# The first slab of the convolution and of the second feed-forward taken from x scaled by its gain, with the token factor and the shift applied to the product

## What is computed

```python
def rms_norm(x, gain):                 # over the features of each token
    return x * rsqrt(mean(x * x, axis=-1) + 1e-6) * gain
def modulate(x, shift, scale):
    return x * (1 + scale) + shift

ax = modulate(rms_norm(hx, norm_mix[1]), sh1, sc1)
b_gate, c_gate, xv = split(ax @ w_in, 3)
hx = hx + g1 * ((b_gate * short_conv(c_gate * xv, w_conv)) @ w_out)
fx = modulate(rms_norm(hx, norm_ffn[1]), sh2, sc2)
hx = hx + g2 * ((silu(fx @ w1) * (fx @ w3)) @ w2)
```

## Time and profile before

| | us |
|---|---|
| median of 3 runs | 2349.04 (2348.41 to 2349.38) |
| the profiled execution | 2346.38 |
| its span | 2344.7 |
| TensorE busy | 2243.8 (96%) |
| VectorE busy | 1129.1 (48%) |
| ScalarE busy | 729.9 (31%) |
| mean granted TensorE clock | 0.979 of full speed |

### The profile page before, as it was taken

The page is one execution under the profiler, slowest core; times in us unless marked ns, Lnnn a source line. Parts: engine busy times, 40 slices in busy tenths (PEclk is TensorE's granted clock), DMA queues, the critical chain, the costliest instruction groups (busy, mean ns, idle before and its releaser), DMA issues.

```text
span 2344.7 us, 25372 instructions
## 1 busy us (share of the span) xinstructions
PE 2243.8 (96%) x9752; PEld 1748.0 (75%) x9752; DVE 1129.1 (48%) x1420; ACT 729.9 (31%) x951; POOL 29.4 (1%) x60
## 2 busy tenths in 40 slices
PE   6999999999899999989989999999999988999996
PEld 4868677686588888868868888887758876878875
DVE  7645343544577333253653323347868647422424
ACT  3221121212343122131233312234555534323321
POOL 0000000000000000000000000000000000000000
PEclk7999999999999999999999999999899999999998
DMA  7232322323187322222212222223201111222220
GB/s 313 72 121 89 121 72 76 120 86 117 61 298 272 108 90 89 92 74 104 90 72 90 100 98 90 89 90 106 72 1 37 37 36 59 102 90 90 90 105 39
DMA packets 32748, 231.88 MB, mean 99 GB/s; under 512 B 3760, under 2 KB 4016, under 8 KB 5552
## 3 DMA queue, kind: packets, MB, share of 16 engines
q1 hardware_dynamic: 23904, 171.98, 20.8%
q0 software_dynamic: 6912, 50.33, 5.7%
q10 hardware_dynamic: 1872, 8.73, 1.0%
HBM read 228.93 MB, written 2.10 MB: 99 GB/s over the span
## 4 chain that ended last, share of the span: by engine, by line
PE 90%; DVE 6%; ACT 2%; issue 1%; DMA 1%; DVEq 0%; POOL 0%; ACTq 0%; POOLq 0%
PE PS L470 26%; PE PS L471 26%; PE PS L472 26%; PE PS L593 4%; PE PS L584 2%; DVE rv L1614 1%; PE PS L848 1%; PE PS L942 1%; PE PS L813 1%; PE PS L932 1%; DVE cv L1967 1%; DMA ada_raw<-ada 1%; DVE w_lo L1511 1%; PE PS L503 0%; PE PS L779 0%
## 5 line engine op out<-in xcount | busy, mean ns | idle before, releaser
L1511 DVE TENSOR_TENSOR w_lo<-raw,w_hi 128x2048 fp32r<-128x2048 f32 x162 | 371.0, 2290 | 670.6 <-ACT w_hi L1072 670.5
L470 PE MATMUL PS<-act_hi,w_hi 128*128 128x512 f32 x1632 | 654.7, 401 | 34.6 <-DVE act_lo L1524 23.4
L1072 ACT ACTIVATE w_hi<-raw 128x2048 fp32r<-128x2048 f32 x162 | 310.1, 1915 | 1105.9 <-PE PS L472 1095.7
L471 PE MATMUL PS<-act_lo,w_hi 128*128 128x512 f32 x1632 | 648.9, 398 | 0.0
L472 PE MATMUL PS<-act_hi,w_lo 128*128 128x512 f32 x1632 | 648.5, 397 | 0.0
L470 PEld LDWEIGHTS PS<-act_hi,w_hi 128*128 128x128 f32 x1632 | 308.8, 189 | 116.6 <-issue 36.9
L471 PEld LDWEIGHTS PS<-act_lo,w_hi 128*128 128x128 f32 x1632 | 308.8, 189 | 76.2 <-issue 1.9
L472 PEld LDWEIGHTS PS<-act_hi,w_lo 128*128 128x128 f32 x1632 | 308.6, 189 | 75.8
L470 PE MATMUL PS<-hid_hi,w_hi 128*128 128x512 f32 (+1 forms) x672 | 266.1, 396 | 0.9 <-ACT sg L1472 0.9
L472 PE MATMUL PS<-hid_hi,w_lo 128*128 128x512 f32 (+1 forms) x672 | 265.4, 395 | 0.0
L471 PE MATMUL PS<-hid_lo,w_hi 128*128 128x512 f32 (+1 forms) x672 | 265.4, 395 | 0.0
(11 more groups left out here) (358 smaller groups left out, 2197.5 us busy)
## 6 DMA issues: line engine op xcount, KB each, us to landing
raw<-slabs SPq DMA_DIRECT2D x162, 1024.0 KB, 4.8
ada_raw<-ada POOLq DMA_DIRECT2D x44, 1024.0 KB, 5.1
early_raw<-ada POOLq DMA_DIRECT2D x4, 1024.0 KB, 21.2
toep<-decay ACTq DMA_DIRECT2D x5, 768.0 KB, 4.2
x<-x_t ACTq DMA_DIRECT2D x1, 2048.0 KB, 9.6
out_t<-x SPq DMA_DIRECT2D x4, 512.0 KB, 2.6
rs<-ctx_t ACTq DMA_DIRECT2D x1, 1024.0 KB, 14.1
con<-consts ACTq DMA_DIRECT2D x1, 642.0 KB, 4.0
```

The lines of the kernel that those rows point to most:

```text
L470: pe.matmul(o, w[0], a[0], start=first, stop=False)
L471: pe.matmul(o, w[0], a[1], start=False, stop=False)
L1072: act.activation(w_hi[:, n % 2, :], raw[:, n % 2, :], ACT.Copy).then_inc(w_hi_done, 1)
L1511: dve.tensor_tensor(w_lo[:, k % 2, :], raw[:, k % 2, :], w_hi[:, k % 2, :].bitcast(F32), ALU.subtract).then_inc(w_lo_done, 1)
```

## The change

For the first slab of the convolution and that of layer 1's feed-forward, the moving operand is no longer the finished normalisation but x times its gain (`xg_hi`, `xg_lo`), which needs no root. Since the token factor `rstd` is common to all features of a token, the product is multiplied by it afterwards. The shift has to go through the same weights: two more moving columns hold it (one would do; two keep the count even), and their result, one value for each output feature, is added as a bias. As 514 columns exceed a bank, each tile is done in two halves of 256 and 258 columns, in two banks. The second slab and all that follow use `act_hi` and `act_lo` as before.

- TensorE: `first_pair` in place of the first turn of `up`. It takes the k in the order in which x is finished. The three sums of squares move from behind the slab before into the first slab, behind its fifth step (`s == KT // 2`), and into bank 6.
- ScalarE: `scaled` (a copy with the gain as scale) ahead of each square. In the first place the rounding of the second slab goes between the last `scaled` and the last square, in the second place ahead of the root. `first_pair` applies the function with the summed shift as bias.
- VectorE: `scaled_rest` behind the additions, and the gains made ahead of them (`block_gain`). `first_pair` copies the shift's sum, multiplies two halves for each tile by `rstd`, and only then makes `w_lo` of the third slab.
- The last output slab of the convolution signals its first tile on its own (`tile_summed`), and its two additions wait for one tile each. `summed` keeps the later counts right.

```diff
+            def first_pair(n, name, order, banks, freed):
+                parts, after_x = 8 * nth_split(name + "_x"), 8 * nth_split(name)
+                pe.wait_ge(w_lo_done, n + 1)
+                pe.wait_ge(banks, freed[0])
+                for s, k in enumerate(order):
+                    pe.wait_ge(lo_ready, parts + s + 1)
+                    for m in range(2):
+                        w = wcols(n, k * 256 + m * P, k * 256 + (m + 1) * P)
+                        for half in range(2):
+                            at = slice(half * H, (half + 1) * H + 2 * half)
+                            mm = product(PS[:, BANK_X[name][m][half], 0:H + 2 * half], w, (xg_hi[:, k, at], xg_lo[:, k, at]),
+                                         s == 0, s == KT - 1)
+                    if s == KT // 2:
+                        pe.wait_ge(banks, freed[2])
+                        gathered_sum(nth(name), 6)
+                mm.then_inc(slab_done, 1)
+                pe.wait_ge(w_lo_done, n + 2)
+                pe.wait_ge(banks, freed[1])
+                tile_pair(n + 1, BANK_X[name][2], act, lo_ready, after_x).then_inc(slab_done, 1)
...
-                up(CONV, KT, FT, parts_of("mix1"))
+                first_pair(CONV, "mix1", FIN, down_added, (KT + 4, KT + 6, KT + 8))
+                up(CONV, KT, FT, parts_of("mix1"), 1)
...
-                swiglu(FFN1, FT + KT, 16, parts_of("ffn1"), None)
+                first_pair(FFN1, "ffn1", range(KT), wout_added, (4 + 6, 4 + 8, 4 + 8))
+                swiglu(FFN1, FT + KT, 16, parts_of("ffn1"), 1)
...
+            def first_pair(n, seen, step, func=ACT.Silu):
+                after_static(n)
+                for m in range(2):
+                    act.wait_ge(x_scaled, step + m + 1)
+                    act.activation(sg[:, m, :], sg[:, m, :], ACT.Identity if func == ACT.Copy else func,
+                                   bias=shift_sum[:, m:m + 1]).then_inc(act_silu, 1)
+                after_static(n + 1)
...
-                norm("mix1", mod_at(1, 0), CONV - 1, FIN, down_added, 8)
-                up(CONV, KT, FT, ACT.Copy)
+                for s, k in enumerate(FIN):
+                    act.wait_ge(down_added, KT + s + 1)
+                    scaled("mix1", s, k)
+                    if s == KT - 1:
+                        after_static(CONV - 1)
+                    square(nth("mix1"), s, x[:, k, :])
+                root(nth("mix1"), T, D, 6)
...
+                    scaled("ffn1", k, k)
                     square(nth("ffn1"), k, x[:, k, :])
-                root(nth("ffn1"), T, D)
                 after_static(FFN1 - 1)
+                root(nth("ffn1"), T, D, 6)
...
+            def first_pair(n, seen, name, conv=False):
+                b = BANK_X[name]
+                dve.wait_ge(slab_done, n + 1)
+                dve.wait_ge(act_silu, seen + 2)
+                for m in range(2):
+                    dve.tensor_copy(shift_sum[:, m:m + 1], PS[:, b[m][1], H:H + 1])
+                    dve.tensor_tensor(sg[:, m, 0:H], PS[:, b[m][0], 0:H], rstd[:, 0:H], ALU.mult)
+                    dve.tensor_tensor(sg[:, m, H:T], PS[:, b[m][1], 0:H], rstd[:, H:T], ALU.mult).then_inc(x_scaled, 1)
+                static_rest(n + 2)
...
+                    if norm and s:
+                        scaled_rest(norm, s - 1, FIN[s - 1])
                     if norm and 2 <= s <= 6:
                         gather(norm, s - 1)
```

More of the change, by code:

```diff
@@ L124, in build @@
         eps = sb("eps", [P, 3])
+        shift_sum = sb("shift_sum", [P, 2])
         std = sb("std", [P, T])
@@ L372, in build @@
         gathered = ("mix1", "ffn1", "post2", "last")
-        split = [q for q in norms if q not in ("final", "post2", "last")]
+        split = ["mix0", "ctx", "ffn0", "mix1_x", "mix1", "ffn1_x", "ffn1", "pre2", "ffn2"]
         def nth(name):
@@ L700, in two_turns, with finish_two_turns @@
                         mm.then_inc(slab_done, 1)
-            def finish_two_turns(n, moving, ready, before, free, norm):
+            def finish_two_turns(n, moving, ready, before, free):
                 for j in range(4):
@@ L1175, in after_static, with scaled, up @@
                     round_slab(n + 2)
-            def up(n, tiles, seen, func=ACT.Silu):
-                with act.Fori(0, tiles // 2) as i:
+            def scaled(name, s, k):
+                g = 3 if name == "mix1" else 4
+                if s == 0:
+                    act.wait_ge(gain_done, g + 2)
+                    at = mod_at(1, 0 if name == "mix1" else 3)
+                    act.activation(xg_hi[:, :, T:T + 2], mod[:, at:at + KT].unsqueeze(2).to_broadcast([P, KT, 2]), ACT.Copy)
+                act.activation(xg_hi[:, k, 0:T], x[:, k, :], ACT.Copy, scale=gain[:, g, k:k + 1]).then_inc(hi_ready, 1)
+            def first_pair(n, seen, step, func=ACT.Silu):
[5 more added lines that the diff above has]
+                after_static(n + 1)
+                for m in range(0 if func == ACT.Copy else 2):
+                    act.wait_ge(hraw_ready, seen + m + 3)
+                    act.activation(hid_hi[:, m, :], hraw[:, m, :], ACT.Copy).then_inc(hid_hi_done, 1)
+            def up(n, tiles, seen, func=ACT.Silu, done=0):
+                with act.Fori(done, tiles // 2) as i:
                     after(n, i)
@@ L1723, in static_rest, with scaled_rest @@
                     rest_slab(n, n)
-            def up(n, tiles, seen, unit0=None, conv=False):
-                with dve.Fori(0, tiles // 2) as i:
+            def scaled_rest(name, s, k):
+                g = 3 if name == "mix1" else 4
+                dve.wait_ge(hi_ready, 8 * nth_split(name + "_x") + s + 1)
+                if s == 0:
+                    at = mod_at(1, 0 if name == "mix1" else 3)
+                    dve.tensor_tensor(xg_lo[:, :, T:T + 2], mod[:, at:at + KT].unsqueeze(2).to_broadcast([P, KT, 2]),
+                                      xg_hi[:, :, T:T + 2].bitcast(F32), ALU.subtract)
+                dve.scalar_tensor_tensor(out=xg_lo[:, k, 0:T], in0=x[:, k, :], scalar=gain[:, g, k:k + 1],
+                                         in1=xg_hi[:, k, 0:T].bitcast(F32), op0=ALU.mult, op1=ALU.subtract).then_inc(lo_ready, 1)
@@ L1728, in up @@
+            def up(n, tiles, seen, unit0=None, conv=False, done=0):
+                with dve.Fori(done, tiles // 2) as i:
                     if unit0 is not None:
```

108 lines of the change are left out of this document (76 added, 32 removed).

## The result

| | before | after |
|---|---|---|
| median, us | 2348.72 (2347.16 to 2349.38, 4 runs) | 2311.02 (2306.89 to 2316.77, 4 runs) |
| profiled execution, us | 2346.38 | 2306.89 |
| its span, us | 2344.7 | 2305.2 |
| mean granted TensorE clock | 0.979 | 0.981 |

The account below looks back on a forecast made before the run. The prediction took TensorE, busy 90% of the span, as the bound, with gains only where it stands still. Savings of 4.5 and 3.65 us in two places made 8.15: median 2349.04 to 2340.9 us, range 2338 to 2346.

Parts of the forecast that it names:

- Part 1: First slab's matmuls in both places: half matmuls 0.118 us apart, 1.42 us a step, 11.3 us a slab.
- rival D: Half matmuls of the first slabs bound by weight loads, 0.233 us apart: slower, 2354.5 us; chance 0.05.
- Part 2: Making `xg_hi` and `xg_lo` on ScalarE and VectorE in both places: cost to TensorE 0 (to 1 us).
- the cover: Second place: moved `w_lo` rounding done 7.7 us after the slab's start, TensorE asks after 11.2: 3.5 us to spare.
- Part 3: Sums behind the fifth step: reciprocal 6.0 and 6.7 us later, idle 2.6 to 2.7 us, then a slower clock costing 1.6.
- Part 4: Before the third slab: six VectorE operations (1.75 us), then `w_lo`; it starts 4.5 and 3.65 us earlier.
- rival E: The six VectorE operations take about 1 us: gain grows 0.75 us in each place, 2339.4 us; chance 0.09.
- Rival B: Clock stays up after the first idle, falls in the second, ahead of the third slab: gain 4.8, 2344.3 us; chance 0.14.
- Rival C: Added VectorE and ScalarE operations cost full durations plus waits between engines: gain 4.1, 2345 us; chance 0.12.
- the sum: Third slab earlier by 4.5 us in the first place and 3.65 in the second, 8.15 in all: median 2340.9 us.

Follow-up runs that it names:

- e2: The changed kernel with `shift_sum` laid into two columns of the existing tile `silu_c`, so no tile moves: 2338.79 us, ratio 0.9962.
- m1: Separate small kernel repeating one slab's product 64 times, moving operand shifted 32 bytes each time, no other engine working: 0.2268 us between matmuls at distance 0.
- m2: Separate small kernel repeating one slab's product 64 times, moving operand shifted 8 bytes each time: slab 10.92 us at distance 0, 11.38 at 168.
- e6: The changed kernel with 128 unused bytes behind `shift_sum`, weights unmoved: 2340.85 us in one run.
- e10: e8 with 224 unused bytes ahead of `act_hi`, making the distance a multiple of 256 bytes: 2289.79 us, ratio 0.9753.
- e9: The kernel before the change with 224 unused bytes ahead of `act_hi`, making the distance a multiple of 256 bytes: 2301.25 us, ratio 0.98.
- e4: The changed kernel with 64 unused bytes behind `shift_sum`, weights unmoved: 2337.11 us in one run.
- e1: The kernel before the change with only an unused tile of 8 bytes where the change puts `shift_sum`: 2326.03 us, ratio 0.9895.
- e3: The changed kernel with 32 unused bytes behind `shift_sum`, weights unmoved: 2338.97 us in one run.
- e8: e2 with the second place's three sums of squares behind the first slab's second step instead of its fifth: 2335.66 us, ratio 0.9947.
- e7: The changed kernel with an unused 32-byte tile ahead of `raw`, moving the weights too: 2308.62 us in one run.
- e5: e2 with an unused 32-byte tile ahead of `raw`, moving every tile including the weights: 2340.36 us in one run.

## Why the prediction was wrong, and where it was right

The table sets the steps of the prediction beside the profile of after, in us from the first slab's start in the first place (1001.74 in the prediction, 988.10 in after).

| step | forecast | measured |
|---|---|---|
| eighth addition done | 6.1 | 6.1 |
| first sum | 7.1 | 7.2 |
| reciprocal starts | 11.6 | 11.5 |
| first `act_lo` starts | 16.5 | 16.4 |
| idle ahead of the second slab | 2.6 | 2.45 |
| last `act_lo` done | 26.8 | 26.7 |
| six VectorE operations | 1.75 | 1.4 |
| third slab starts | 30.9 | 30.6 |

Part 1 held. In the first place five steps of 12 half matmuls took 995.29 - 988.10 = 7.19 us, 0.120 each, for a forecast of 0.118; with the weights loaded for each half, there was no sign of rival D. The Trainium skill (TensorE: Matmul & The Clock Gate, section LDWEIGHTS) has a weight load take as long as its columns need. Its 107 ns, an estimate by that page, lie under these 120 ns, so the trace doesn't contradict it, and no run here shows the load's time by itself (its own row lasts 0.19 us).

Part 2 held to the tenth in the first place; in the second TensorE never waited for the rest of the weights that was moved (its only wait for `w_lo` is the one shown), so the cover held. Part 3 held: the last half matmul starts at 1002.82 and the second slab at 1005.39, which less the half matmul's own 0.12 is an idle of 2.45 us (2.29 where the trace takes the modelled end), and behind it the clock did fall in after's first place, to 0.64 of full speed in the next 4 us:

```profile
1002.80:1005.40 2.60, 0.31 (x4) 0.14 (x2) 2.40 (x5) 1.39 (x2) 0.00 (x0) 1.00 0.22 91
1005.40:1009.40 4.00, 4.00 (x12) 3.10 (x13) 3.93 (x6) 1.88 (x3) 0.00 (x0) 0.64 0.00 0
1018.70:1022.00 3.30, 3.28 (x14) 2.73 (x15) 2.78 (x3) 1.47 (x1) 0.00 (x0) 1.00 0.65 226
```

Part 4 held in the first place, with `w_lo` as the last to come. In the second place `w_lo` is out at 1202.94 and ScalarE's second SiLU at 1202.97, and the trace puts the wait down to that: the two came closer together than forecast (0.4 us). The six operations were 0.3 to 0.4 us cheaper, about half of the way to rival E. Rival B (the clock falls in the second idle) did not come: in after that idle is 0.5 us, and the clock is 1.00 behind it (last row). Nor did it come where its condition was met: where the clock stayed at 1.00 after the first idle (seven places, see the last section), the second idle was 1.7 us and the clock stayed at 1.00 behind that too. Rival C (operations at full durations) did not come either.

The step that failed stands in the sum: 4.5 + 3.65 = 8.15, as though nothing else in the kernel could change. It has no term for the pace of the 7200 other matmuls. The prediction took 0.233 to 0.235 from the earlier trace rows and used it as a constant of the engine, for the slabs of the changed kernel too. That number belonged to the distance at which the tiles of before happened to stand, and the line `shift_sum = sb("shift_sum", [P, 2])` moved them. The missing term was 7200 x 0.0044 = 32 us, four times all that was in the sum. By itself the change is worth 8 to 9.5 us, as e2 shows, where the prediction had worked out 8.15 from the chain.

Nothing in the rows of before could have given that term: one kernel shows one distance. A reader of the diff could have seen that a tile was added ahead of all operands of TensorE, and kept a wider range.

## What to carry to other kernels

The distance from the weights to the moving operand in a partition's memory, modulo 256 bytes, is a setting of its own: for products of 512 columns place both at the same remainder (for 256 columns that was the slowest of the places seen here, see below), and look at the spacing of matmuls in a stretch where TensorE never stops. When a change adds or resizes a tile, compare that spacing ahead of the changed code first, and time the change also with the tiles where they were: here three quarters of the measured gain had nothing to do with the idea. A local gain read from the chain of waits was good to 0.4 us in each place (4.5 and 3.65 forecast, 4.82 and 4.01 measured), but only for what hangs on the chain.

## What the runs showed of the hardware

- The spacing of matmuls with fp32r operands (the type of the `_hi` and `_lo` tiles) of 512 columns, each with its own weight load, is 0.2268 us at distance 0 modulo 256 bytes (m1), 0.2289 (after) to 0.2291 (m1) at 64, 0.2313 to 0.2360 at the others (m2, in steps of 8 bytes) but for 168, where it is 0.2370, all at granted clock 1.00. The Trainium skill (SBUF — State Buffer, section A bandwidth-pool intuition that's wrong) gives TensorE a second, independent read port for weight loads. If that meant that the two reads never disturb each other, the distance should not matter, and the measurement decides: it does. Why (both reads meeting in some part of the memory would be a guess), and whether it needs a weight load with each matmul, no run shows.
- The spacings of the scan don't carry over to every product. For the 576 matmuls with the weights as moving operand the distance turns round: 224 in before, 192 in after, 64 in e6 and 0 in e10. They are at 0.2333 or 0.2334 in the first three, so 64 gives them nothing, and at 0.2269 in e10. The 192 products of 256 columns of the context go the other way: 0.1169 us apart in before, 0.1156 in after, and 0.1198, the slowest, in e9 and e10 at distance 0.
- The faster pace at distance 64 isn't always held. At 128 (e4) the spacing isn't constant either: 0.2324 up to 1200 us, 0.2333 from there to 1550, and both again later. The four runs of after fall in two groups (2306.89 and 2307.67; 2314.36 and 2316.77), those of e1 too (2318.02; 2325.14 to 2326.95). In the profiled execution of e1 the spacing was 0.2333 from about 610 to 970 us and 0.2289 behind it:

```profile
700.00:800.00 100.00, 100.00 (x430) 81.03 (x429) 56.92 (x73) 31.33 (x27) 5.30 (x10) 1.00 0.55 200
...
880.00:980.00 100.00, 100.00 (x431) 80.98 (x430) 28.10 (x21) 23.28 (x21) 0.00 (x0) 1.00 0.27 94
1280.00:1380.00 100.00, 100.00 (x438) 82.04 (x438) 29.16 (x22) 28.79 (x26) 0.00 (x0) 1.00 0.27 95
```

  360 us of it cost 1540 x 0.0044 = 6.8 us, which is about the distance between the groups; that the other runs of the longer groups have this reason is not shown, as they have no trace. What switches it is open. At distance 0 the runs of e10 lie within 1.3 us.
- An idle of TensorE of 2.45 us doesn't always cost the clock. It comes in 16 places of the nine profiled kernels with the change. In nine of them (both of after, e3 and e4, the first of e2 and e8, the second of e7) the clock was 0.57 to 0.68 over the next 4 us; in seven (both of e5 and e6, the first of e7 and e10, the second of e2, here) it stayed at 1.00:

```profile
1207.00:1211.00 4.00, 3.99 (x17) 3.09 (x18) 3.93 (x6) 1.86 (x3) 0.00 (x0) 1.00 0.00 0
```

  The third slab started no earlier for it (1220.34 - 1189.78 = 30.56 us after the first, for 30.57 in after): VectorE's chain sets it, and the matmuls only wait more ahead of it.
